# Seven block products in place of eight for the attention projections of the later head pairs, in a hybrid retention and attention block

## The reference, cut to what matters

```python
# SEQ 256 rows, D_MODEL 2048, 8 retention heads and 8 attention heads of 128 columns
h   = rms_norm(x, norm1_g)
proj = h @ w_in                      # retention q,k,v,gate and attention q,k,v of every head
ret = head_group_norm(retention(rotary(rq), rotary(rk), rv)) * silu(rg)
att = chunk_attention(rms_norm(aq), rms_norm(ak), av, rel_bias)
x   = x + concat([ret, att]) @ w_out
h   = rms_norm(x, norm2_g)
x   = x + square(relu(h @ w_ff1)) @ w_ff2
```

## Time and profile before

| | us |
|---|---|
| median of 3 runs | 1105.57 (1105.01 to 1106.1) |
| the profiled execution | 1104.85 |
| its span, first to last instruction | 1103.1 |
| TensorE busy | 1097.7 |
| VectorE busy | 857.8 |
| ScalarE busy | 695.4 |

### The profile page before, as it was taken

One profiled execution on the slowest core, in us unless ns is written; L12 is line 12 of the kernel. 1 busy time (PEld: TensorE's weight loads), 2 busy tenths in 40 slices (PEclk: granted clock), 3 DMA queues, 4 the chain that ended last, 5 costly groups with the idle time before them and its releaser, 6 DMA issues.

```text
span 1103.1 us, 13129 instructions
## 1 busy us (share of the span) xinstructions
PE 1097.7 (100%) x5190; PEld 932.3 (85%) x5190; DVE 857.8 (78%) x803; ACT 695.4 (63%) x827; POOL 53.4 (5%) x69
## 2 busy tenths in 40 slices
PE   9999999999999999999999999999999999999998
PEld 9789989989988888888888888888888888888887
DVE  7876876866866678869778879778869787869784
ACT  6964664674674555777655677655677655577662
POOL 0100100100100000000000000000000000000000
DMA  9975774775776647878788787797787787787792
GB/s 360 306 255 173 206 254 170 198 263 173 191 277 217 242 178 198 263 264 239 226 297 229 252 282 218 233 299 221 254 284 214 243 290 222 261 277 221 245 279 93
DMA packets 43965, 263.81 MB, mean 239 GB/s; under 512 B 4864, under 2 KB 7680, under 8 KB 16256
## 3 DMA queue, kind: packets, MB, share of 16 engines
q1 hardware_dynamic: 37712, 220.61, 53.7%
q0 software_dynamic: 5760, 41.95, 20.3%
q10 hardware_dynamic: 432, 0.41, 0.1%
HBM read 260.85 MB, written 2.10 MB: 238 GB/s over the span
## 4 chain that ended last, share of the span: by engine, by line
PE 95%; ACT 0%; DVE 0%; issue 0%; DVEq 0%
PE acc L931 10%; PE acc L927 10%; PE acc L929 10%; PE acc L797 7%; PE acc L810 7%; PE acc L804 7%; PE bankC L889 4%; PE acc L889 4%; PE bankC L882 4%; PE acc L882 4%; PE acc L884 4%; PE bankC L884 4%; PE acc L624 2%; PE acc L629 2%; PE acc L636 2%; PE bankD L889 1%
## 5 line engine op out<-in xcount | busy, mean ns | idle before, releaser
L1779 DVE TENSOR_TENSOR w_lo<-raw,w_hi 128x2048 fp32r<-128x2048 f32 x180 | 410.8, 2288 | 126.8 <-ACT w_hi L1300 126.5
L1300 ACT ACTIVATE w_hi<-raw 128x2048 fp32r<-128x2048 f32 x180 | 344.7, 1916 | 220.0 <-PE acc L931 146.6
L1497 DVE TENSOR_TENSOR w_lo<-raw,w_hi 128x1024 fp32r<-128x1024 f32 (+1 forms) x150 | 164.9, 1110 | 47.5 <-ACT w_hi L1053 47.4
L1053 ACT ACTIVATE w_hi<-raw 128x1024 fp32r<-128x1024 f32 (+1 forms) x150 | 140.6, 965 | 21.6 <-DVE raw L1506 12.6
L797 PE MATMUL acc<-w_hi,hT_hi 128*128 128x384 f32 (+1 forms) x408 | 104.3, 374 | 0.1
L927 PE MATMUL acc<-w_hi,hF_hi 128*128 128x512 f32 x256 | 100.8, 394 | 0.0
L931 PE MATMUL acc<-w_hi,hF_lo 128*128 128x512 f32 x256 | 99.7, 390 | 0.0
L929 PE MATMUL acc<-w_lo,hF_hi 128*128 128x512 f32 x256 | 99.6, 389 | 0.0
L804 PE MATMUL acc<-w_hi,hT_lo 128*128 128x384 f32 (+1 forms) x408 | 97.7, 357 | 0.0
L810 PE MATMUL acc<-w_lo,hT_hi 128*128 128x384 f32 (+1 forms) x408 | 97.2, 356 | 0.0
L927 PE MATMUL acc<-w_hi,dF_hi 128*128 128x512 f32 x248 | 96.9, 391 | 0.0
(11 more groups left out here) (276 smaller groups left out, 1798.9 us busy)
## 6 DMA issues: line engine op xcount, KB each, us to landing
raw<-in_w_up SPq DMA_DIRECT2D x64, 1024.0 KB, 6.5
raw<-in_w_down SPq DMA_DIRECT2D x64, 1024.0 KB, 6.5
raw<-in_w_ret SPq DMA_DIRECT2D x32, 1024.0 KB, 5.7
raw<-in_w_att SPq DMA_DIRECT2D x28, 768.0 KB, 4.5
raw<-in_w_out SPq DMA_DIRECT2D x16, 1024.0 KB, 4.8
raw<-in_w_up POOLq DMA_DIRECT2D x16, 1024.0 KB, 8.8
raw<-in_w_down POOLq DMA_DIRECT2D x16, 1024.0 KB, 9.1
raw<-in_w_ret POOLq DMA_DIRECT2D x8, 1024.0 KB, 9.0
```

What stands on the lines that cost most here:

```text
L1053: nc.scalar.activation(piece(w_hi, q, 0, n), raw[:, r, half * n:(half + 1) * n], ACT.Copy).then_inc(hi_done, 1)
L1300: nc.scalar.activation(w_hi[:, ring(s)], raw[:, r, :], ACT.Copy).then_inc(slab_hi, 1)
L1497: nc.vector.tensor_tensor(piece(w_lo, q, 0, n), raw[:, IN_PLAN[i, READ_AT.get(step, step)][0], half * n:(half + 1) * n], piece(w_hi, q, 0, ...
L1779: nc.vector.tensor_tensor(w_lo[:, ring(s)], raw[:, r, :], w_hi[:, ring(s)].bitcast(f32), ALU.subtract).then_inc(slab_lo, 1)
```

## The change

In pairs 1 to 3 the two attention heads are computed like the retention heads: slabs 2 and 3 direct (I2, I3 and J2, J3), slabs 0 and 1 of both heads by seven products, written in small letters (q1 p5 p6 p7 p3 q2 p4), with blocks A, B, D, E. Pair 0 stays as it was. The steps of a later pair's attention are laid among the retention steps of the pair before and of its own. D, the third attention slab, is loaded ahead of H1 and H2 (the retention pair's last two blocks); its sum is made in two halves.

```diff
...
-    "I0 I1 I2 I3 J0 Q1 J1 P5 J2 P6 J3 P7 P3 Z1 Q2 Z2 P4 H1 H2".split()] * (BLOCKS - 1)
...
-    "I0 I1 I2 I3 J0 a b J1 J2 d J3 Z1 e Z2 H1 H2".split()] * (BLOCKS - 1)
...
+IN_ORDER = [(0, step) for step in "I0 J0 I1 J1 I2 Q1 J2 P5 I3 P6 J3 P7 P3".split()]
+for _i in range(1, BLOCKS + 1):
+    _r, _here = "Z1 Q2 Z2 P4 H1 H2", "Z1 Q2 q1 Z2 P4 p5 H1 p6 H2 p7 p3 I2 q2 Q1 I3 p4 P5 J2 P6 J3 P7 P3"
+    _loads = "Z1 e A Z2 B D H1 H2 I2 E a I3 b J2 d J3" if _i < BLOCKS else "Z1 e Z2 H1 H2"
...
             def att_proj(h):
-                    act.wait_ge(xc_lo, 3 * SLAB_KT)
+                    act.wait_ge(xc_lo, KT)
+                elif h % 2 == 0:
+                    act.wait_ge(r_qk_ok, h)
...
-                        wide = N if fresh else n
+                        wide = N if fresh and i == 0 else n
...
+            def in_sum_half(n, other, read, half):
+                r, o, width = pair_raw(n, "a")[0], pair_raw(n, other), PIECE_KT * pair_cols(n)
+                cols = slice(half * width, (half + 1) * width)
+                dve.wait_ge(in_raw[o[0]], o[1])
+                dve.wait_ge(lo_done, pair_first(n, read) + half + 1)
+                ins = nc.vector.tensor_tensor(raw[:, r, cols], raw[:, r, cols], raw[:, o[0], cols], ALU.add)
+                if half:
+                    ins.then_inc(in_summed, 1)
...
             def add_b(n):
+                pool.wait_ge(in_summed, 2 * n + 1)
+                add_second(n, "b", 1, in_b)
+            def add_e(n):
+                pool.wait_ge(lo_done, pair_first(n, "P6") + 2)
+                add_second(n, "a", 0, in_e)
```

The places of the attention heads' work on TensorE:

```diff
-                for h, places in ((2 * i, (13, 15, 20, 22) if i else (23, 25, 27, 28)),
-                                  (2 * i + 1, (27, 28, 31, 33) if i else (30, 31, 34, 35))):
+                places = ((23, 25, 27, 28), (29, 31, 34, 36))[second] if i == 0 else (
+                    (35, 37, 41, 43), (46, 48, 51, 53))[second]
```

The places on ScalarE that the prediction speaks of:

```diff
-                    at_piece(i, 8, att_proj, h)
-                    at_piece(i, 9, att_squares, h)
+                at_piece(i, 30, att_proj, h)
+                at_piece(i, 31, ret_scale, u + 1)
+                at_piece(i, 31, att_squares, h)
+                at_piece(i, 33, ret_mix, u + 1)
```

And on VectorE:

```diff
-                    at_piece(i, 9, in_sum, i, "b", "Q1")
-                    at_piece(i, 11, att_norm, h)
-                    at_piece(i, 14, in_sum, i, "d", "P5")
+                at_piece(i, 3, in_sum, n - 1, "b", "Q1")
+                at_piece(i, 8, in_sum_half, n - 1, "d", "P5", 0)
+                at_piece(i, 9, in_sum_half, n - 1, "d", "P5", 1)
+                at_piece(i, 25, in_sum, n, "b", "Q1")
+                at_piece(i, 33, in_sum, n, "d", "P5")
+                at_piece(i, 34, att_norm, h)
```

More of the change, by code:

```diff
@@ L508, in _ @@
             load_decay(1)
[L509 to L519, removed]
+            for i, name in IN_LOADS[11:]:
+                load_in(i, name)
+                if name == "D":
+                    load_bias(i)
+                elif name == "J3":
+                    load_decay(2 * i)
+                    load_decay(2 * i + 1)
             load_group(G_OUT, w_out, 0, N)
@@ L565, in ret_power, with add_second @@
                 nc.gpsimd.tensor_tensor(r_rs[:], r_ve[:], neg_half[:, 0:MT], ALU.pow).then_inc(r_rs_ok, 1)
[L567 to L570 removed]
+            def add_second(n, into, c, done):
+                table, cols = w_att if n % 2 else w_ret, SLAB_KT * pair_cols(n)
+                row = pair_row(n, c, 1)
+                nc.gpsimd.dma_start(raw[:, pair_raw(n, into)[0], 0:cols], table[row:row + P, :],
@@ new lines, in _ @@
+            nc.gpsimd.tensor_tensor(rstd1[:], me[:], neg_half[:, 0:MT], ALU.pow).then_inc(rstd1_ok, 1)
+            att_power(0)
+            mask_bias(0)
+            add_e(0)
+            att_power(1)
+            for i in range(1, BLOCKS):
+                add_b(2 * i - 1)
+                add_e(2 * i - 1)
+                ret_power(2 * i - 2)
+                mask_bias(i)
+                add_b(2 * i)
+                ret_power(2 * i - 1)
+                att_power(2 * i)
+                add_e(2 * i)
@@ L636, in group @@
                             mm = nc.tensor.matmul(acc[par][m][:, 0:n], hi[:, k, tile_cols(m)],
-                                                  piece(w_lo, j, t * n, (t + 1) * n), start=False, stop=last)
+                                                  piece(w_lo, q, t * n, (t + 1) * n), start=False, stop=last)
                         if j == PIECES - 1 and m == 0:
@@ L846, in _ @@
                     f()
-            work = {j: work.get(8 * G_OUT + j, []) for j in range(PIECES)}
+            work = {j: work.get(IN_PIECES + j, []) for j in range(PIECES)}
             work[2] = work[2] + [lambda: pe.wait_ge(a_mix_lo, HEADS)]
@@ L1264, in _ @@
-            for q in range(8 * G_OUT):
+            at_piece(0, 12, keep_in_q1, 0)
+            at_piece(0, 16, keep_in_p5, 0)
+            at_piece(0, 18, att_proj, 0)
+            at_piece(0, 20, att_squares, 0)
+            at_piece(0, 22, att_proj, 1)
+            at_piece(0, 23, att_qT, 0)
+            at_piece(0, 24, set_y, 0)
+            at_piece(0, 25, set_h, 0)
+            at_piece(0, 25, att_squares, 1)
+            at_piece(0, 26, att_exp, 0)
+            at_piece(0, 27, att_pT, 0)
@@ new lines, in _ @@
+            i, u = BLOCKS, HEADS - 2
+            at_piece(i, 6, ret_proj, u)
+            at_piece(i, 8, ret_tanh, u)
+            at_piece(i, 9, ret_qT, u)
+            at_piece(i, 12, ret_proj, u + 1)
+            at_piece(i, 12, ret_scale, u)
+            at_piece(i, 13, ret_mix, u)
+            at_piece(i, 12, ret_tanh, u + 1)
+            at_piece(i, 13, ret_qT, u + 1)
+            at_piece(i, 16, ret_scale, u + 1)
+            at_piece(i, 17, ret_mix, u + 1)
+            for q in range(IN_PIECES):
@@ L1275, in _ @@
                     f()
-            group(G_OUT, N, N, {j: work.get(8 * G_OUT + j, []) for j in range(PIECES)})
+            group(G_OUT, N, N, {j: work.get(IN_PIECES + j, []) for j in range(PIECES)})
             def hi_slab(s):
```

476 lines of the change are left out of this document (248 added, 228 removed).

## The result

The changed kernel takes 1110.2 us (median of five runs, 1110.08 to 1112.42) where the kernel before takes 1105.57. The ratio is 1.0051, 95% interval 1.0039 to 1.0063. Forecast were 1105.0 us and a range of 1098.0 to 1108.5. The profiled execution is the longest of the five, 1112.42 us, with a span of 1110.3 and a mean granted clock of 0.995; three of the five runs lie at 1110.1 to 1110.2 with a clock of 0.997. The other two, at 1112.0 and 1112.4, have a clock of 0.995; that step of 2 us turned out to be the key.

A forecast was written before the change was run, and what follows sets the result against it. TensorE bounds the kernel, busy 1097.7 of 1103.1 us. Saving -7.4, waits +6.4 and smaller places +0.5 sum to -0.5, so the median goes from 1105.57 to 1105.0 us; range 8 in 10, 1098.0 to 1108.5.

The forecast's parts named there:

- What the change takes from TensorE: Pairs 1 to 3: fewer matmuls and no 512-wide bank openings save 2.48 us a pair, 7.4 us for three.
- What it adds elsewhere: Extra VectorE and ScalarE work and DMAs in later pairs fit on average: VectorE 70.5, ScalarE 57 of 81 us.
- The place where it doesn't hold: Transposes of `a_qk`, later pair's first head: TensorE arrives at 9.2 us, they start at 11.35; 2.1 us wait, 6.4 for three.
- zero: In a later pair, the moment TensorE starts p4, when I3's last piece is done; the wait is timed from it.
- the walk: Later pair followed piece by piece; its eleven-term chain through ScalarE and VectorE to `a_qk` put the transposes at 11.35 us.
- Smaller places: First pair's second-head transposes 0.45 us once, pair 1's retention rotation 0.2, gaps before Z1 closing up to 0.5 a pair.
- three small terms: Second-head transposes, retention rotation and gaps before Z1, taken as cancelling, with -1.5 and +1.5 us kept for the range.
- The clock: Rival: waits drop the clock for the following P6 step, 2.8 us more three times, 1113.3 us; chance 0.04.
- The late slab: Rival: retention block b lands late, VectorE's sum and I3's low part wait, 2.4 us more a pair, 1112.2; chance 0.12.
- No or short waits: Rival: the `a_qk` transposes don't wait, 1098.1 us, or wait 1 us each, 1101.1; chance 0.24.

The follow-up runs named there:

- fillers: Ten or five matmuls whose result nobody reads, ahead of the three late `a_qk` transposes, added to the changed kernel: 1108.2 us with ten, 1107.79 with five.
- the moved line: Changed kernel with VectorE making `a_qk` of each later pair's first head directly behind the slab sum and retention low part: 1103.1 us, ratio to before 0.9977.

## Why the prediction was wrong

*What the change takes from TensorE, 7.4 us: right.* A pair without its wait measures 81.05 us of 83.52 before, 2.47 a pair; forecast was 2.48.

*What it adds elsewhere: right.* VectorE 70.2 us of a pair (70.5 forecast), ScalarE 57.3 to 57.5 (57), DMA share 0.72 to 0.74 ("under 0.8").

*The place where it doesn't hold: right in place, a little short in size.* TensorE arrived 9.26 us after zero (forecast 9.2). `a_qk` ended at 11.8 in pair 1 (11.3): the half microsecond is there by the start of the sum, at 6.58 in place of 6.05. Of it 0.22 is the landing of slab d, and 0.3 is VectorE's own queue: the walk let J2's second low part start as soon as its high part was there, but it stands behind the first low part and the mean squares and ends at 6.35. Gaps 2.6, 2.3 and 2.3 in place of three times 2.1: +0.8 us.

*Smaller places: mis-sized.* The second head's transposes in the first pair wait 0.3 us (67.06 to 67.37; forecast 0.45). The rotation of the first retention head in pair 1 was put at 0.2 us; it is 0.87, and 0.20 more for a low part just ahead of it. VectorE has a half sum of the attention, the rotation's three operations, two low parts and a small one ahead of `r_qk`, and the 0.2 was given without a sum of them. The prediction calls its three small terms cancelling and yet carries +0.5 in the sum, with a bound of +1.5; these places brought +1.4.

*The clock: the step that failed.* "2.1 us in one piece has no row" was right, and the right conclusion would have been that a forecast wait far longer than any gap in the trace has an unknown price, with both bounds in the sum. Instead the sum priced the wait at its bare length and the clock at nothing, and the fall went to a rival at 0.04. The profiles show two or three falls in the changed kernel, 3.2 to 4.9 us, and the mean clocks of its other runs (0.997 or 0.995) fit two or three; without them it would stand at an estimated 1107.8, within the forecast range. Its size was off too, the other way: 2.8 us for the whole P6 step, 1.6 measured, since the clock comes back before that step is over. The Trainium skill, page "TensorE: Matmul & The Clock Gate", section "Why this matters for your kernels", warns of idle gaps between bursts. The traces here agree with its direction, but not with its bound, which is longer: here gaps of 2.1 to 2.6 us were enough in most cases, and the measurement decides.

Shown by runs: the wait costs its length and the clock 1.6 us a fall, apart from each other (fillers, and the moved line). With matmuls in the gaps and no falls it stands at 1107.8 to 1108.2 us, still slower than before by 0.2%: the three gaps alone, 7.2 us, eat the gain. *The late slab*: refuted, in no profile does TensorE wait for a load or for the low part of I3; VectorE's sum waits 0.2 to 0.5 us for slab d in pair 1 of six profiles, which comes out in the gap. *No or short waits, 1098.1 to 1101.1*: this is what the kernel would be worth with its order mended; 1101.9 was reached.

Still open: why one gap of 2.13 to 2.58 us brings the clock down and another of the same length doesn't. In the profiles with such waits (2.13 to 2.63 us) 11 of 14 did, and one of 1.56 us.

## What to carry to other kernels

A wait that you forecast on an engine that has been busy without a break is dearer than its length: look for a gap of that length in the trace, and if there is none, put the clock's share in the sum and not only among the rivals. When a wait ends on an instruction of another engine, ask what stands in that engine's queue ahead of it that it doesn't need; here one line in the table of places turned +4.6 us into -2.6. And before moving the waiting step out of the way, see what its wait covers: here it covered weights that were late as well.

## What the runs showed of the hardware

TensorE, busy before and behind at 2.4 GHz, went to 1.2 GHz behind waits of 2.1 to 2.6 us in 11 of 14 cases, behind 3.56 to 3.76 us in three of three, and behind 1.30 to 1.58 us in one of five, for about 3 us (once for over 6, from within the gap on), at 1.3 to 2.6 us of lost time (mostly 1.6). Behind waits of 0.84 to 1.27 us the profiles show 1.00. Whether it falls differs from one execution to the next of the same program at the same instruction, which makes runs of one kernel scatter in steps (1110.1 and 1112.2 us; 1106.2 to 1109.0). Independent matmuls put into such a gap kept the clock up: five or ten of them in each of three places took 2.0 to 3.2 us off, by which of the two measurements of the changed kernel they are held against.
